# Forget attention on a head's own 64 rows, with an 8-row choice of the forget row and no clearing

## What is computed

```python
def fox_attend(q, k, v, Fq, Fk, q_pos, k_pos):
    s = jnp.einsum('bqhd,bkhd->bhqk', q, k).astype(jnp.float32) * (HEAD_DIM ** -0.5)
    s = s + jnp.swapaxes(Fq, 1, 2)[..., :, None] - jnp.swapaxes(Fk, 1, 2)[..., None, :]
    s = jnp.where(k_pos[None, :] <= q_pos[:, None], s, -jnp.inf)
    p = jax.nn.softmax(s, axis=-1)
    return jnp.einsum('bhqk,bkhd->bqhd', p.astype(v.dtype), v)
```

## Time and profile before

| | us |
|---|---|
| median of 3 runs | 2089.11 |
| lowest and highest | 2088.52, 2090.69 |
| span of the profiled execution | 2085.8 |
| PE, DVE, ACT, POOL busy | 1640.9, 1353.0, 660.6, 811.2 |
| DMA, mean over the span | 352 GB/s |

### The profile page before, as it was taken

The page is one execution under the profiler, slowest core; times in us unless marked ns, Lnnn a source line. Parts: engine busy times, 40 slices in busy tenths (PEclk is TensorE's granted clock), DMA queues, the critical chain, the costliest instruction groups (busy, mean ns, idle before and its releaser), DMA issues.

```text
span 2085.8 us, 25868 instructions
## 1 busy us (share of the span) xinstructions
PE 1640.9 (79%) x8180; PEld 872.9 (42%) x8180; DVE 1353.0 (65%) x3075; ACT 660.6 (32%) x1940; POOL 811.2 (39%) x604
## 2 busy tenths in 40 slices
PE   6999988887977996666799676679968777776776
PEld 4546446544654552343355233235513433221232
DVE  4246866564458876656887665688757567674764
ACT  2111222121124452323355232335523333332332
POOL 0188672213014443434354243435424334343442
PEclk9999999898988998898799889879988999998999
DMA  8378645886679999999999999999999999999996
GB/s 296 108 259 279 226 146 165 305 270 211 196 274 416 401 416 413 413 415 421 383 404 421 412 414 415 421 377 400 421 377 368 415 419 420 420 421 397 422 422 285
DMA packets 169993, 733.43 MB, mean 352 GB/s; under 512 B 17757, under 2 KB 18606, under 8 KB 103154
## 3 DMA queue, kind: packets, MB, share of 16 engines
q0 software_dynamic: 75024, 545.82, 63.6%
q1 hardware_dynamic: 94834, 185.96, 26.0%
HBM read 722.69 MB, written 9.12 MB: 351 GB/s over the span
## 4 chain that ended last, share of the span: by engine, by line
PE 38%; DMA 33%; DVE 14%; issue 5%; ACT 4%; SPq 3%; POOL 3%; DVEq 0%; POOLq 0%; ACTq 0%
PE bank L479 37%; DMA R<-in_peer_uv,R 19%; DMA R<-in_w_out 5%; DMA RING<-in_peer_uv,R 4%; DVE RING L2107 2%; DVE R L2107 2%; SPq L2360 2%; DMA R<-in_peer_wq 2%; PE bank L486 1%; DMA R<-h2s_d 1%; ACT R L1336 1%; SPq L2419 1%; POOL R L2346 1%; DMA R<-in_cache_v 1%; POOL MV L2271 1%
## 5 line engine op out<-in xcount | busy, mean ns | idle before, releaser
L2346 POOL DMA_INDIRECT RING<-in_peer_uv,R x390 | 437.6, 1122 | 708.8 <-PE bank L479 572.7
L479 PE MATMUL bank<-RING,R 128*64 128x512 f32 (+2 forms) x1560 | 516.8, 669 | 229.6 <-ACT R L1336 216.6
L479 PE MATMUL bank<-R 128*128 128x128 f32 (+6 forms) x2216 | 400.2, 378 | 91.8 <-ACT R L1336 79.3
L2107 DVE SCALAR_TENSOR_TENSOR RING<-RING,MV 128x1024 f32<-128x1024 f32 x288 | 351.1, 1222 | 170.9 <-DMA RING<-in_peer_uv,R 161.0
L479 PEld LDWEIGHTS bank<-R 128*128 128x128 f32 (+3 forms) x2216 | 259.0, 184 | 254.7 <-issue 243.0
L479 PEld LDWEIGHTS bank<-RING,R 128*64 128x64 f32 (+2 forms) x1560 | 158.2, 160 | 494.1 <-issue 474.8
L1346 ACT ACTIVATE R<-R 128x2 f32<-128x2 f32 x256 | 51.9, 203 | 772.3 <-DVE RING L2107 618.3
L2346 POOL DMA_INDIRECT R<-in_peer_uv,R x130 | 152.1, 1170 | 229.3 <-PE bank L479 212.0
L2107 DVE SCALAR_TENSOR_TENSOR R<-R,MV 128x1024 f32<-128x1024 f32 x96 | 117.4, 1223 | 60.3 <-DMA R<-in_peer_uv,R 58.6
L2107 DVE SCALAR_TENSOR_TENSOR RING<-RING,R 128x1024 f32<-128x1024 f32 x96 | 117.2, 1221 | 55.5 <-DMA RING<-in_peer_uv,R 51.3
L479 PEld LDWEIGHTS bank<-HT,R 128*128 128x128 f32 x1024 | 127.0, 201 | 56.1 <-issue 54.9
(11 more groups left out here) (321 smaller groups left out, 1818.8 us busy)
## 6 DMA issues: line engine op xcount, KB each, us to landing
R<-in_peer_wq SPq DMA_DIRECT2D x16, 2048.0 KB
RING<-in_w_mod SPq DMA_DIRECT2D x12, 2048.0 KB, 8.1
MV<-in_cache_k SPq DMA_DIRECT2D x88, 256.0 KB, 3.8
R<-in_cache_v SPq DMA_DIRECT2D x84, 256.0 KB, 3.7
R<-in_w_out SPq DMA_DIRECT2D x6, 2048.0 KB
MV<-in_cache_v SPq DMA_DIRECT2D x44, 256.0 KB, 3.9
RING<-in_w_in SPq DMA_DIRECT2D x5, 2048.0 KB, 9.8
R<-in_cache_k SPq DMA_DIRECT2D x40, 256.0 KB, 3.7
```

The costliest lines, as they stand in the source:

```text
L479: i = nc.tensor.matmul(out, lhsT, rhs, start=start, stop=stop, **k)
L2107: V.scalar_tensor_tensor(u, u, 1.0, H2HIGH if s_ % 2 and n < PAIRED * PH else H2[n // PH % 2], ALU.mult, ALU.mult, accum_out=DOT[:, n % 4, ...
L2346: nc.gpsimd.indirect_dma_start(UV[g % UN], None, a["peer_uv"][0], bass.IndirectOffsetOnAxis(ap=idx, axis=0)).then_inc(S(f"uv_in{g % UN}"), 16)
```

## The change

The score product uses the head's own 64 rows of FQ and FK, the choice of the forget row 8 rows of the identity and 8 of FORGET, which all lies in HT now. FQO and the five clearing operations of GpSimd are gone, and with them the waits for fox_zero. TensorE turns the tails after the scores of unit 0 and the log values in unit 1; forget_sums moves to unit 3. VectorE does the tails' copies in unit 0, forget_turned in unit 1, the new scores in unit 2, the copies of forget_after in unit 3, the 15 additions in units 4 to 7 and the last one in unit 8. On the sync queue chunk(12) goes ahead of sconv_load(1).

```diff
-        FQO = part(HFLAT, 2048, 2048, j=4, t=SEQ)
-        FORGET = [MV[:, 2, 256:384], HFLAT[:, 256:512], MV[:, 2, 384:768], HFLAT[:, 512:1024]]
+        FORGET = [HFLAT[0:8, 2048:2176], HFLAT[0:8, 256:512], HFLAT[0:8, 2176:2560], HFLAT[0:8, 512:1024]]
...
-                if u == 0:
-                    pe.wait_ge(S("fox_zero"), 5)
...
-                mm(b[:, 0:w], (FQO if h % 2 else FQ)[:, h // 2, i * P:(i + 1) * P], FK[:, h // 2, 0:w], True, False)
-                mm(b[:, 0:w], ident[:, h:h + 1].to_broadcast([P, P]), FORGET[i][:, 0:w], False, False)
+                r, j = head_of(h)
+                mm(b[:, 0:w], FQ[r, j, i * P:(i + 1) * P], FK[r, j, 0:w], True, False)
+                mm(b[:, 0:w], ident[0:8, h:h + 1].to_broadcast([8, P]), FORGET[i][:, 0:w], False, False)
                 mm(b[:, i * P:w], ident[:, :], hide_q[:, :], False, True, full(("sc", u)))
...
-            steps = {1: forget_sums, 10: sample_max_turn, 12: sample_max_spread, 16: sample_sums}
+            steps = {0: tail_turns, 1: forget_turns, 3: forget_sums, 10: sample_max_turn, 12: sample_max_spread, 16: sample_sums}
...
-            act.wait_ge(S("fox_zero"), 2)
...
+            def forget_pages(late, early_):
+
+                for g in range(late, early_ - 1, -1):
+                    settle()
                     step(V.tensor_tensor(TP[:, :, :, g], TP[:, :, :, g], TP[:, :, :, g + 1], ALU.add))
...
-            between = {1: forget_after, 9: sample_scores, 11: sample_max, 13: sample_shift, 15: sample_exp_sums, 17: sample_probs, 26: first_squares, 30: lambda: norm_sums(0), 32: srule_gate, 33: lambda: norm_scale(0)}
+            between = {0: tails_out, 1: forget_turned, 2: new_scores, 3: forget_after, 4: lambda: forget_pages(14, 12), 5: lambda: forget_pages(11, 9),
+                       6: lambda: forget_pages(8, 5), 7: lambda: forget_pages(4, 0), 8: forget_total, 9: sample_scores, 11: sample_max, 13: sample_shift, 15: sample_exp_sums, 17: sample_probs, 26: first_squares, 30: lambda: norm_sums(0), 32: srule_gate, 33: lambda: norm_scale(0)}
...
             sample_conv(0)
-            job_done(pool, ("gv", 4))
-            pool.wait_ge(S("kred"), 32)
-            nc.gpsimd.memset(MV[:, 2, 256:768], 0.0).then_inc(S("fox_zero"), 1)
-            nc.gpsimd.memset(HFLAT[:, 256:1024], 0.0).then_inc(S("fox_zero"), 1)
-            pool.wait_ge(S("logf_pages"), 16)
-            pool.wait_ge(S("fox_zero"), 2)
-            nc.gpsimd.tensor_copy(FQO[64:P, :, :], FQ[64:P, :, :]).then_inc(S("fox_zero"), 1)
-            pool.wait_ge(S("fox_zero"), 3)
-            nc.gpsimd.memset(FQO[0:64, :, :], 0.0).then_inc(S("fox_zero"), 1)
-            pool.wait_ge(S("fox_zero"), 4)
-            nc.gpsimd.memset(FQ[64:P, :, :], 0.0).then_inc(S("fox_zero"), 1)
-            pool.wait_ge(S("fox_zero"), 5)
-
             sample_conv(1)
...
             sconv_load(0)
             chunk(11)
+            chunk(12)
             sconv_load(1)
-            chunk(12)
             sconv_load(2)
             sp.wait_ge(S("kred"), 32)
             bmod(4)
```

More of the change, by code:

```diff
@@ L634, in _, with tail_turns @@
                 forget_rows(i)
[L635 to L639, removed]
+            def tail_turns():
+                pe.wait_ge(S("tails"), 12)
+                for q in range(3):
+                    b = take_bank(("tail", q), "D")
+                    for j in range(4):
+                        tr(b[0:3, j * P:(j + 1) * P], TAILI[:, q * 4 + j, :], full(("tail", q)) if j == 3 else None)
             def forget_turns():
@@ L647, in forget_turns @@
                         tr(b[:, m * P:(m + 1) * P], LG.rearrange("p (n h) -> p h n", h=HEADS)[:, h, :], full(("lp", half)) if m == 3 else None)
-            forget_turns()
             def head_of(h):
@@ L1172, in _ @@
                 if i:
-                    A(FORGET[i][0:8, 0:i * P], b[0:8, 0:i * P], ACT.Copy).then_inc(S("forget_cols"), 1)
+                    A(FORGET[i][:, 0:i * P], b[0:8, 0:i * P], ACT.Copy).then_inc(S("forget_cols"), 1)
                     act.wait_ge(S("forget_cols"), i)
-                A(FORGET[i][0:8, i * P:(i + 1) * P], b[0:8, i * P:(i + 1) * P], ACT.Copy, scale=-1.0).then_inc(free(("frow", i)), 1)
+                A(FORGET[i][:, i * P:(i + 1) * P], b[0:8, i * P:(i + 1) * P], ACT.Copy, scale=-1.0).then_inc(free(("frow", i)), 1)
             job_done(act, ("cvT", 11))
@@ L1613, in _, with tails_out, new_scores @@
             conv_tokens(11)
[L1614 to L1626, removed]
+            def tails_out():
+                for q in range(3):
+                    b = full_bank(dve, ("tail", q))
+                    V.tensor_copy(TAILO[0:3, q * 512:(q + 1) * 512], b[0:3, :]).then_inc(S("tail_out"), 1)
+                    dve.wait_ge(S("tail_out"), q + 1)
+                    dve.sem_inc(free(("tail", q)), 1)
+            def new_scores():
+                dve.wait_ge(S("sample_ready"), 1)
+                T8 = CACC[0:NB, 0, :]
+                dve.wait_ge(S("decays"), 3)
+                step(V.scalar_tensor_tensor(small[:, 786:818], small[:, 300:332], -1.0, small[:, 690:722], ALU.mult, ALU.mult))
+                step(V.tensor_tensor(T8, PS[0:NB, COL_FQ:COL_FQ + 512], PS[0:NB, COL_FK:COL_FK + 512], ALU.mult))
+                settle()
+                V.tensor_reduce(SN[0:NB, :], T8.rearrange("p (h d) -> p h d", h=8), AXX, ALU.add).then_inc(S("new_score"), 1)
             def fox_max(u):
@@ L1717, in forget_after, with forget_total @@
                     job_read(dve, ("ltot", half))
-                for g in range(14, -1, -1):
+            def forget_pages(late, early_):
+                for g in range(late, early_ - 1, -1):
+                    settle()
                     step(V.tensor_tensor(TP[:, :, :, g], TP[:, :, :, g], TP[:, :, :, g + 1], ALU.add))
-                    settle()
+            def forget_total():
+                settle()
                 step(V.tensor_tensor(flat(LP[:, :, :, 0:15]), flat(LP[:, :, :, 0:15]), flat(TP[:, :, :, 1:16]), ALU.add))
@@ L1796, in first_squares @@
                 dve.sem_inc(S("sq_free"), 1)
-            between = {1: forget_after, 9: sample_scores, 11: sample_max, 13: sample_shift, 15: sample_exp_sums, 17: sample_probs, 26: first_squares, 30: lambda: norm_sums(0), 32: srule_gate, 33: lambda: norm_scale(0)}
+            between = {0: tails_out, 1: forget_turned, 2: new_scores, 3: forget_after, 4: lambda: forget_pages(14, 12), 5: lambda: forget_pages(11, 9),
+                       6: lambda: forget_pages(8, 5), 7: lambda: forget_pages(4, 0), 8: forget_total, 9: sample_scores, 11: sample_max, 13: sample_shift, 15: sample_exp_sums, 17: sample_probs, 26: first_squares, 30: lambda: norm_sums(0), 32: srule_gate, 33: lambda: norm_scale(0)}
             between.update(zip(SRULE_AT, (srule_norms, srule_scale, srule_new, srule_state, srule_out)))
-            forget_turned()
             def sample_heads_at(z):
```

## The result

The change makes the kernel slower: 2113.94 us against 2089.11, a ratio of 1.0107 with the 95% interval [1.0081, 1.0132]. A second measurement of the same kernel (run e12) gave 2115.15 against 2088.81, 1.0124 [1.0109, 1.0140]. The profiled execution has a span of 2119.7 us and is the slowest of its five: the two traces differ by 33.9 us, the medians by 24.8.

What follows compares the result with a forecast made beforehand. It took GpSimd's clearing, VectorE's queue and DMA landings as the bound, then the DMA-held tail from 615 us. Terms +0.1 +1.7 +0.8 = +2.6, say 2.5, on span 2085.8; 3.3 to the median gave 2091.6, range 2085.0 to 2097.0.

Steps and rivals of the forecast that it cites:

- The start of unit 0: First attention unit, without GpSimd's clearing ahead of it: begins at about 301.8, some 5.7 us sooner.
- the bias as a new stall: VectorE before mod_row(4): bias rows land at 319.5, wanted at 311.7, a new stall of about 8 us.
- the whole lead: The 5.7 us gained at unit 0, forecast to be gone by unit 4's maximum, leaving +0.1 us.
- The page sums: VectorE, units 4 to 8: 7.4 us of adds make sample_scores 1.7 us late, at 347.2; bounds -1.8 and +5.
- free switches: Score units on TensorE: the assumption that changing the products' array shape costs 0 each.
- The unit's products: TensorE, each unit: fewer rows save nothing; shape changes cost 0.13 us each, 0.4 a unit, 12.8 in all.
- What is queued behind it: VectorE and TensorE after mod_row(4): slow-clock restart and queued copies take unit 4's maximum to +0.1 us.
- Where the 0.4 counts: Later units: VectorE, then TensorE's 13 idle us, hide switching except in units 30 and 31; +0.8 us.
- The tail: From 615 us, DMA engines 99% busy: carries any earlier shift to the end one for one.
- Dear switches: Rival, chance 0.20: shape changes cost 0.25 to 0.3 us each, TensorE bounds units 4 to 17; slower, 2097.
- Cheap switches: Rival, chance 0.20: shape changes in the units cost 0 each; +0.9 us in all, 2090.0.
- No new wait: Rival, chance 0.15: bmod(4) lands before delaying anybody, the earlier start counts in full; -6 us, 2083.

Runs made afterwards that it cites:

- e12: The changed kernel again, word for word, measured beside the other runs on the same chip; 2115.15 us, ratio 1.0124 to the kernel before.
- e1: Changed kernel with the forget-row choice over 128 rows again, scores still on 64, bias late; 2090.42 us, ratio 1.0008 to the kernel before.
- e2: Changed kernel with scores and choice both on 128 rows, bias late, heads not kept apart (timing only); 2087.49 us, ratio 1.0011 to the kernel before.
- e3: Changed kernel with scores on 128 rows, choice still on 8, bias late, heads not kept apart (timing only); 2093.92 us, ratio 1.0013.
- e4: Changed kernel, narrow products kept, with bmod(4) and bmod(5) issued before sconv_load(1); 2095.09 us, ratio 1.0056 to the kernel before.
- e6: Changed kernel with both products on 128 rows and the bias issued early, heads not kept apart (timing only); 2077.92 us, ratio 0.9947.
- e5: Kernel before with only the two products narrowed to 64 and 8 rows, clearing, waits and order kept; 2128.53 us, ratio 1.0198.

## Why the prediction was wrong

It said 2091.6, no measurable change, and gave slower 0.24. The time lies above the range.

**Right.** The start of unit 0 (302; measured 301.19), the bias as a new stall (mod_row(4) at 319.5; 319.29), the bank of mod_row(4) stopping TensorE (from about 315 to 320.8; 5.34 us up to 320.63), and with it the loss of the whole lead. The page sums, which I put at 1.7 us with VectorE as the bound, come out near that where the clock is left out of it: sample_scores starts at 346.34 in e1 and at 345.30 in e2, against my 347.2, or 346.4 for free switches. In the change itself it starts at 354.86.

**The step that failed** is "The unit's products". I priced narrow rows by columns and shape changes alone. The shape change was a little too small, 0.13 each for 0.4 a unit; the trace after has 0.5 a unit at the high clock. That is not the miss: e1 and e3 show that 0.2 to 0.4 a unit is hidden. What was missing is the clock. In "What is queued behind it" and "The page sums" I let TensorE be back at full speed before unit 4 because it had taken 6 us in the kernel before, and I let it stay there. With narrow products it took until 339.4, and the clock fell again at 346.3, 356.5 and 377.0, the first and the last time without any idle time ahead. So a unit's work cost up to 4.58 us for 1.94.

**What followed from it.** "Where the 0.4 counts" relied on 13 idle us of TensorE behind the sync queue's list. They were eaten by the clock (2.8 are left), TensorE became the bound of the samples' value stage (busy 57.2 of 60 us), and the lateness grew from 9.4 us at sample_scores to 29.8 at the first gather. The tail carried it on, as said, and added 4 in this execution. A small slip besides: the 3.3 us that I put between span and median are about 2 that every execution has (2121.84 for a span of 2119.7) and 1.3 of scatter.

**The rivals.** "Dear switches" had the sign and 2097, by a mechanism that the runs refute. "Cheap switches" falls by the 0.5 us a unit. "No new wait" is what e4 makes, narrow products and all: I gave it 2083, 6 us below the kernel before, and it is at 2095.09, 0.6% above. Only with full rows as well (e6) does the wait's end give a gain, 10 us at the median. The rule of the Trainium skill that I weighed, "TensorEngine Tiling (Array Packing)", Key Properties, is a drain of the engine at each change of the tiling mode. The trace agrees with it by the 0.5 us a unit, but that isn't what made the kernel slow.

Taken apart by ratios: the order of units without clearing, -0.5% (e6); the late bias, +0.6% (e2 less e6); the narrow products, +1.0% (the change less e2), or +1.1% with the early bias (e4 less e6). The three steps lead from the kernel before over e6 and e2 to the change, so they add up to its +1.1% by construction. Each is a difference of two ratios that are known to about 0.2%. With the narrow products taken first (e5, +2.0%) the shares would be others, since wait and clock act on each other.

## What to carry to other kernels

A product that needs only 8 or 64 rows is not cheaper on them, and it can slow all of TensorE's work around it: look at the granted clock of a stretch beside its busy time, and where a busy TensorE runs at its lower clock, give the products their full rows (zeros will do) before looking for waits. When work is moved ahead on one engine, go through what the sync queue holds in front of each input of the moved work; here two bias loads behind a convolution's buffer cost 0.6% (e2 less e6), and moving them was one edit. And once a start comes sooner, the next thing in that queue is late: after the bias it was the weight chunk of unit 8.

## What the runs showed of the hardware

TensorE's granted clock doesn't follow busy time alone. With products on 64 and 8 rows it fell to 0.50 at 346.3 us behind more than 6 us in which TensorE was busy all the time, where the kernel before kept 1.00 over an idle stretch of 2.24 us; and 17 us of products on 128 rows added to the change raised the mean of 320 to 500 us from 0.68 to 0.86 and took 13 us off the kernel. The Trainium skill, "TensorE: Matmul & The Clock Gate", Part 1, says that the clock follows how busy the engine has been. By this case's rows that is not all: the choice on 8, 32 and 128 rows gave kernels of 2114, 2098 and 2090 us. What it is about few rows that counts stays open. The change's five runs spread from 2100.6 to 2121.8, and the mean clock of a run goes with its time (0.903 for the fastest, 0.892 for the slowest).
